# Encoder layer on one core: a reordered front, two decay buffers, raw router transposes, and the rows of an expert laid over all partitions

## The reference

```python
# x: (1, 512, 1024) for each sequence, mem: (1, 256, 1024)
P = rms_norm(x, norm_mix) @ w_in          # z, xbc, dt, q, k, v, pool columns
x = x + concat(ssd_heads, neighbourhood_attention, pool) @ w_out
x = x + memory_cross_attention(rms_norm(x, norm_xa), rms_norm(mem, norm_mem))
x = x + hier_moe(rms_norm(x, norm_ffn))
```

## Time and profile before

| what | value |
|---|---|
| median of 3 runs | 1175.89 us (1174.95 to 1176.49) |
| the profiled execution | 1172.96 us |
| its span in the trace | 1170.9 us |
| mean granted TensorE clock | 0.938 |
| busy PE, PEld | 1016.6, 810.3 us |
| busy DVE, ACT, POOL | 784.6, 466.5, 294.0 us |
| chain that ended last, by engine | PE 42%, DVE 13%, DMA 12%, issue 9%, ACT 6% |
| DMA | 197.40 MB, mean 169 GB/s |

### The profile page before, as it was taken

One profiled execution on the slowest core, in us unless ns is written; L12 is line 12 of the kernel. 1 busy time (PEld: TensorE's weight loads), 2 busy tenths in 40 slices (PEclk: granted clock), 3 DMA queues, 4 the chain that ended last, 5 costly groups with the idle time before them and its releaser, 6 DMA issues.

```text
span 1170.9 us, 13975 instructions
## 1 busy us (share of the span) xinstructions
PE 1016.6 (87%) x5029; PEld 810.3 (69%) x5029; DVE 784.6 (67%) x1251; ACT 466.5 (40%) x849; POOL 294.0 (25%) x346
## 2 busy tenths in 40 slices
PE   5798898998898999999979999756999998889982
PEld 4576676867677778788867888655777766666661
DVE  4436776777677677873455676457988787877771
ACT  4123343323235423421233343234666565564640
POOL 2223214321341222200110111004355233232212
PEclk9898999897898989899989999867999999999997
DMA  6132223121131523315120112735999989999952
GB/s 228 46 108 63 81 90 120 46 81 55 47 103 65 174 82 127 108 63 198 43 72 18 55 55 104 310 136 196 351 368 371 372 349 372 344 357 343 350 209 85
DMA packets 63397, 197.40 MB, mean 169 GB/s; under 512 B 16417, under 2 KB 22977, under 8 KB 50913
## 3 DMA queue, kind: packets, MB, share of 16 engines
q1 hardware_dynamic: 43344, 152.73, 35.9%
q0 software_dynamic: 18688, 39.52, 9.5%
q10 hardware_dynamic: 1296, 4.26, 0.9%
HBM read 190.16 MB, written 37.75 MB: 195 GB/s over the span
## 4 chain that ended last, share of the span: by engine, by line
PE 42%; DVE 13%; DMA 12%; issue 9%; ACT 6%; POOL 3%; ACTq 0%; POOLq 0%; DVEq 0%
DMA edr<-w_e_down 11%; PE bank L946 7%; PE bank L947 7%; PE bank L948 7%; PE gu_ps L946 3%; PE gu_ps L948 3%; PE gu_ps L947 3%; PE y_ps L1327 2%; PE bank L1131 2%; DVE egl L1728 2%; PE bank L1013 2%; PE xg_ps L1292 1%; ACT dec L1573 1%; ACT prob L1591 1%; PE bank L1263 1%
## 5 line engine op out<-in xcount | busy, mean ns | idle before, releaser
L946 PE MATMUL bank<-Wh,hTh 128*128 128x512 f32 x384 | 159.2, 415 | 7.9 <-issue 6.7
L947 PE MATMUL bank<-Wl,hTh 128*128 128x512 f32 x384 | 154.2, 401 | 0.0
L948 PE MATMUL bank<-Wh,hTl 128*128 128x512 f32 x384 | 153.9, 401 | 0.0
L1728 DVE TENSOR_TENSOR egl<-egr,ghi 128x2048 fp32r<-128x2048 f32 x64 | 143.9, 2288 | 14.7 <-ACT ghi L1397 14.7
L1397 ACT ACTIVATE ghi<-egr 128x2048 fp32r<-128x2048 f32 x64 | 119.6, 1931 | 0.0
L946 PE MATMUL gu_ps<-ghi,xgH 128*128 128x512 f32 x256 | 104.3, 408 | 1.4 <-DVE xgL L2093 1.4
L948 PE MATMUL gu_ps<-ghi,xgL 128*128 128x512 f32 x256 | 101.2, 395 | 0.0
L947 PE MATMUL gu_ps<-egl,xgH 128*128 128x512 f32 x256 | 100.9, 394 | 0.0
L946 PEld LDWEIGHTS bank<-Wh,hTh 128*128 128x128 f32 x384 | 75.5, 197 | 24.4 <-issue 7.4
L948 PEld LDWEIGHTS bank<-Wh,hTl 128*128 128x128 f32 x384 | 74.9, 195 | 16.6
L947 PEld LDWEIGHTS bank<-Wl,hTh 128*128 128x128 f32 x384 | 75.1, 196 | 15.6 <-issue 0.5
(11 more groups left out here) (325 smaller groups left out, 2243.3 us busy)
## 6 DMA issues: line engine op xcount, KB each, us to landing
egr<-w_e_gate SPq DMA_DIRECT2D x32, 1024.0 KB, 20.7
egr<-w_e_up SPq DMA_DIRECT2D x32, 1024.0 KB, 23.7
edr<-w_e_down SPq DMA_DIRECT2D x32, 1024.0 KB, 24.3
raw<-w_in SPq DMA_DIRECT2D x50, 256.0 KB, 3.1
xn<-w_in SPq DMA_DIRECT2D x22, 256.0 KB, 3.0
x_sb<-x_prompt SPq DMA_DIRECT2D x8, 512.0 KB, 6.1
partial_rows<-x_sb ACTq DMA_DIRECT2D x8, 512.0 KB, 2.6
ffn_rows<-xn_ffn POOLq DMA_DIRECT2D x8, 512.0 KB, 2.9
```

Of the source, the lines that this page charges most:

```text
L946: pe.matmul(dst, ah, bh, start=first, stop=False)
L947: pe.matmul(dst, ah, bl, start=False, stop=False)
L948: return pe.matmul(dst, al, bh, start=False, stop=last)
L1728: tt(egl[n % 4][:, a, :, :], egr[n % 4][:, a, :, :], ghi[n % 2][:, a, :, :].bitcast(F32), ALU.subtract)\
```

## The change

In words: (1) At the start the gain is loaded behind the first weight, hT 1 stands before norm 3 and hT 3 within the first head step; TensorE's wait for the constants moves to dtp 0. (2) Of a convolution ScalarE does the first product (from the bank, semaphore `conv_in`), and the tanh with the last product becomes a step `act` behind the next convolution; the steps around them are put in another order, and dt is split in two. (3) `dec` gets a second buffer where the attention's probabilities lie, with two new waits for that place; sdec is two chunks ahead; xdt and the normalisation (`yn`) are steps of their own; gating stands before the state's update. (4) The gain for xa shares the semaphore of mem. (5) The router's transposes read `x_sb` before normalisation; `router_w` is multiplied once by the gain, the logits by `rs`; the end of the loop is in another order, and VectorE copies the last half of `hf`. (6) The one-hot rows compare with `iota_s`, by which rank r goes to partition 8 (r mod 16) + r div 16.

```diff
-                   ("norm", "mix", 2), ("w", U_QK, 2), ("norm", "mix", 3), ("w", U_QK, 3)]
-            tl += [("hT", "mix", i) for i in range(1, TPS)]
+                   ("norm", "mix", 2), ("w", U_QK, 2), ("hT", "mix", 1), ("norm", "mix", 3), ("w", U_QK, 3),
+                   ("hT", "mix", 2)]
...
+            heads[0].insert(1, ("hT", "mix", 3))
...
-        mixed([[u[0]], [conv[4], na1[0]], [conv[5], conv_t[4]] + (ssd_groups(s - 1)[-1] if s else []),
-               [na2[0], u_t[0], u[1], nav[0]]], quarters(u0 + U_XS))
-        mixed([[na1[1], conv[0]], [conv[1], conv_t[0], na2[1]]], quarters(u0 + U_Z))
-        tl += [u_t[1], ("dtv", s), norm[0], conv[2], nav[1], conv_t[1], na1[2], norm[1], conv[3], conv_t[2]]
-        mixed([[z[0], h_t[0], na2[2]], [z[1], h_t[1], norm[2], nav[2], na1[3]],
-               [z[2], h_t[2], ("dt", s), conv_t[3], norm[3], na2[3]], [z[3], ("sback", s, 3), nav[3], h_t[3]]],
+        act = [("act", s, m) for m in range(6)]
+        mixed([[u[0], na1[0]], [conv[4]], [act[4], conv[5], conv_t[4]] + (ssd_groups(s - 1)[-1] if s else []),
+               [act[5], na2[0], u_t[0], u[1], nav[0]]], quarters(u0 + U_XS))
+        mixed([[na1[1], conv[0]], [act[0], conv[1], conv_t[0], na2[1]]], quarters(u0 + U_Z))
+        tl += [act[1], norm[0], conv[2], conv_t[1], nav[1], act[2], na1[2], norm[1], conv[3], conv_t[2], u_t[1], ("dtv", s)]
+        mixed([[z[0], act[3], h_t[0], na2[2], ("dtw", s)], [z[1], h_t[1], norm[2], nav[2], na1[3], ("dt", s)],
+               [z[2], conv_t[3], h_t[2], norm[3], na2[3]], [z[3], ("sback", s, 3), nav[3], ("sback", s, 2), h_t[3]]],
...
+        else:
+            tl += [("hT", "ffn", i - 1), ("xsn", i + 1)] + ranked[:1] + [("norm", "ffn", i - 1), ("xo", i), ("router", i - 1)]
+            tl += ranked[1:]
+    i = NT - 1
+    tl += [("xs2", i), ("hT", "ffn", i - 1), ("xav", i), ("topk", i - 2), ("norm", "ffn", i - 1), ("router", i - 1),
+           ("rank", i - 2), ("slots", i - 2), ("pre", 0), ("topk", i - 1), ("xo", i), ("rank", i - 1), ("hT", "ffn", i),
+           ("slots", i - 1), ("norm", "ffn", i), ("router", i), ("pre", 1), ("topk", i), ("rank", i), ("slots", i)]
...
-    back = [[("sback", s, 1), dec[0]]]
-    return back + [[y[0]], [dec[1], out[0]], [y[1]], [dec[2], out[1]], [y[2]], [dec[3], out[2]], [y[3]], [out[3]]]
+    groups = [[("sback", s, 1), dec[0], x[0]], [dec[1]]]
+    for c in range(TPS):
+        groups.append([y[c]] + x[c + 1:c + 2])
+        groups.append([yn[c]] + dec[c + 2:c + 3] + [out[c]])
...
+        decays = [dec, nc.alloc_sbuf_tensor_at("dec1", [P, 2, SSD_H, P], F32, offset=at["prob"])]
...
-                if step == ("norm", "mix", 0):
+                if step == ("w", U_QK, 0):
                     sp.dma_start(gain[:, :], row(dram["norm_mix"], D)).then_inc(gain_ld["mix"], 16)
...
-                if kind == "init":
+                if step == ("dtp", 0):
                     pe.wait_ge(const_ld, 16 * N_CONST)
...
+                    if st == "ffn":
+                        pe.wait_ge(x2, 2 * i + 2)
+                    src = x_sb[:, i, :] if st == "ffn" else normed(st, i)
...
+                    act.activation(cacc[:, k % 2, :], pb(step)[:, :], ACT.Identity, scale=cwh[:, m, 1:2],
+                                   bias=cbh[:, m:m + 1]).then_inc(conv_in, 1)
...
+                        if step[1] == 0:
+                            wait_full(act, ("sy", SEQS - 1, TPS - 1), 0)
...
+                    if step == ("norm", "ffn", 0):
+                        tt(router_w[:, :, :], router_w[:, :, :], per_head(g_ffn, NL), ALU.mult).then_inc(router_g, 1)
...
-                    link(ts(acc, b[:, :], cwh[:, m, 1:2], cbh[:, m:m + 1], ALU.mult, ALU.add))
+                    dve.wait_ge(conv_in, k + 1)
...
+                    if c == 1:
+                        wait_full(dve, ("nav", s, 3))
...
+                    if s and m == 0:
+                        wait_full(dve, ("sy", s - 1, TPS - 1), 0)
...
-                    tt(logits[:, i, :], pb(step)[:, 0:NL], router_b[:, :], ALU.add).then_inc(is_free(step), 1)
+                    stt(logits[:, i, :], pb(step)[:, 0:NL], rs[:, k:k + 1], router_b[:, :], ALU.mult, ALU.add)\
...
-                        ins = ts(oneh_p[:, c * NT + i, :], iota_p[:, :], rk[:, c, i:i + 1], None, ALU.is_equal)
+                        ins = ts(oneh_p[:, c * NT + i, :], iota_s[:, :], rk[:, c, i:i + 1], None, ALU.is_equal)
...
+                        pool.iota(iota_s[:, :].rearrange("p (a b) -> p a b", a=16), [[1, 16], [16, 8]], base=0,
+                                  channel_multiplier=0, allow_small_or_imprecise_dtypes=True).then_inc(r_pool, 1)
...
-                elif kind == "hT" and step[1] == "ffn":
-                    i = step[2]
+                elif kind == "router":
+                    i = step[1]
                     pool.wait_ge(xn_done, 1 + nth("norm", "ffn", i))
                     pool.dma_start(hn_dram[i * P:(i + 1) * P, :], xn_ffn[:, :]).then_inc(hn_st, 16)
```

More of the change, by code:

```diff
@@ L56 @@
 N_INIT = 8
-N_RPOOL = 5
+N_RPOOL = 6
 ROUND = 2.0 ** 23
@@ L166, in ssd_groups @@
 def ssd_groups(s):
-    dec, y, out = ([(kind, s, c) for c in range(TPS)] for kind in ("sdec", "sy", "sout"))
-    back = [[("sback", s, 1), dec[0]]]
-    return back + [[y[0]], [dec[1], out[0]], [y[1]], [dec[2], out[1]], [y[2]], [dec[3], out[2]], [y[3]], [out[3]]]
+    dec, x, y, yn, out = ([(kind, s, c) for c in range(TPS)] for kind in ("sdec", "xdt", "sy", "yn", "sout"))
+    groups = [[("sback", s, 1), dec[0], x[0]], [dec[1]]]
+    for c in range(TPS):
+        groups.append([y[c]] + x[c + 1:c + 2])
+        groups.append([yn[c]] + dec[c + 2:c + 3] + [out[c]])
+    return groups
 def bank_uses(step):
@@ L630, in encoder_layer @@
         init_a = sem("init_a")
-        gain_ld = {st: sem(f"gain_ld_{st}") for st in ("mix", "mem", "xa", "ffn")}
+        gain_ld = {st: sem(f"gain_ld_{st}") for st in ("mix", "mem", "ffn")}
         conv_sum = sem("conv_sum")
+        conv_in = sem("conv_in")
         conv_th = sem("conv_th")
@@ L1130, in _ @@
                         for dr in range(2):
-                            last = pe.matmul(b[:, hc], dec[:, dr, h, :], xdt[:, dr, hc], start=dr == 0, stop=dr == 1)
+                            last = pe.matmul(b[:, hc], decays[c % 2][:, dr, h, :], xdt[:, dr, hc], start=dr == 0, stop=dr == 1)
                     last.then_inc(is_full(step, 0), 1)
@@ L1445, in _ @@
                         dst = normed(st, i)
-                        if before_it:
+                        if st == "xa" and before_it:
                             wait_full(act, before_it[-1], 1)
-                        else:
+                        elif not (st == "ffn" and i):
                             wait_raw_used(act, plan.last_in[2 if st == "xa" else 3])
@@ L1463, in _ @@
                     i = step[2]
-                    for half in range(2):
+                    for half in range(1 if i == NT - 1 else 2):
                         wait_full(act, step, half)
@@ L1822, in _ @@
                     ins.then_inc(conv_sum, 1)
+                elif kind == "act":
+                    m, k = step[2], nth("conv", *step[1:])
                     dve.wait_ge(conv_th, k + 1)
@@ L1889, in _ @@
                         link(tt(y1[:, :], y1[:, :], y2[:, :], ALU.add))
+                        wait_full(dve, step, 0)
+                        tt(y1[:, :], y1[:, :], pb(step, 0)[:, :], ALU.add).then_inc(is_free(step, 0), 1)
+                        wait_released(dve, step, 0)
+                        dve.wait_ge(z_ld, 16 * (k + 1))
+                        tt(y1[:, :], y1[:, :], zg[:, :], ALU.mult).then_inc(y_done, 1)
                     j = 3 if kind == "sy" else 0
@@ L1908, in _ @@
                         wait_released(dve, step, j)
[L1909 to L1919 removed]
+                elif kind == "yn":
+                    dve.wait_ge(yrs_done, nth(*step) + 1)
+                    for g in range(SSD_G):
+                        r = slice(256 * g, 256 * g + 256)
+                        ins = ts(y2[:, r], y1[:, r], yrs[:, g:g + 1], None, ALU.mult)
+                    ins.then_inc(yn_done, 1)
                 elif kind == "sdec":
@@ L2299, in _ @@
                         wait_mixed(pool)
-                    pool.dma_start(GAIN[step[1]][:, :], bass.AP(dram[name].tensor, 0, [[0, P], [1, D]])).then_inc(gain_ld[step[1]], 16)
+                    pool.dma_start(GAIN[step[1]][:, :], bass.AP(dram[name].tensor, 0, [[0, P], [1, D]])).then_inc(gain_ld["ffn" if step[1] == "ffn" else "mem"], 16)
                     if step[1] == "ffn":
@@ L2358, in _ @@
                     ins.then_inc(u_win, 1)
+                    pool.wait_ge(u_win, 1 + nth(*step))
                 elif kind == "uT":
```

94 lines of the change are left out of this document (46 added, 48 removed).

## The result

The changed kernel takes 1140.41 us (median of four runs, 1137.49 to 1148.31) against 1176.19 (four runs, 1174.95 to 1177.24): a ratio of 0.9709 with a 95% interval of 0.9666 to 0.9752, faster by 35.8 us. The forecast was 1108 with a range of 1082 to 1136: right sign, half the size, outside the range.

What follows compares the result with a forecast made beforehand. It took TensorE to bound the kernel, busy 1016.6 of 1170.9 us, with its waits and lowered clock to gain. 7.5 + 22 + 16 + 4 + 12 + 6 = 67.5 off 1172.96, plus 2.93 to the median, gave 1108 us; range 1082 to 1136.

Steps and rivals of the forecast that it cites:

- Start, 7.5: Kernel start: TensorE's initial wait of 6.66 us and 2 of clock saved, less about 1 waiting for hT 3: 7.5 us.
- The 0 for the gain's DMA: Start: loading the gain one weight later costs 0, plus or minus 1, as the first transposes wait anyway.
- Convolution and attention, 22: Convolutions and neighbourhood attention, twice: lighter VectorE work and an earlier first softmax save 22 us, between bounds 10 and 37.
- What is late next is VectorE: Convolutions and attention: VectorE's softmaxes share its queue, and ScalarE's new first product stands before exponentials that others wait for.
- VectorE's 18 us of relief: Convolutions: VectorE loses 9.7 + 8.4 = 18 us, from products moved to ScalarE and tanh waits filled with other work.
- Chunks, 16: SSD chunks, twice: decay two chunks ahead removes L1131's 12.9 us wait; half of the upper bound 32 counted, 16 us.
- The 2 us of clock: TensorE: each wait of over 2 us costs 2 us more, since work behind it runs at a lower clock.
- Rival B: Before the experts VectorE becomes the bound; convolutions give 10, chunks 6: 1130 us. Chance 0.21.
- Loop and tail, 16: Router: transposes no longer wait for normalisation; 4 us in the loop and 12 in the tail.
- Experts, 6: Experts: the new row places fill the engines used evenly, 0.3 us x 19 = 6 us; half of the places stay empty.
- The 108%: Experts: load if all rows sat on eight engines, 67.2 + 40.4; taken to say nearly all rows do.
- The upper bound of 27: Experts: rows perfectly spread over the engines save 1.4 us for each of 19 experts, 27 us.

Runs made afterwards that it cites:

- the groups were undone: Changed kernel with nine chunk groups in the old arrangement (y and its normalisation in one group), second decay buffer kept: 1123.22 us, ratio 0.9581.
- the old places: Changed kernel with an expert's rank r on partition r again: 1144.97 us, ratio 0.9755.
- a true spread: Changed kernel with the iota placing rank r on DMA engine r mod 16, so 64 rows are four on each of 16 engines: 1106.24 us, ratio 0.9438.

## Why the prediction was wrong, point by point

- **Start, 7.5.** Right in kind; measured 10.2 and 11.0. No wait is left at the first q/k projections, and in the first 60 us the clock is 1.00 instead of 0.94. The 0 for the gain's DMA did not hold: the first normalisation waits for the gain until 8.98 us, where it began at 6.67, and the first transposes come 2.3 us later. The first projection still starts 2.4 us earlier (18.88 for 21.25), since three transpose steps stand in front of it and not four.
- **Convolution and attention, 22.** The term that was mis-sized. Leads of 8.5 and 5.2 us (9.5 and 5.4 in the second profile) make 14 to 15, of which 2.9 and 4.8 go at the backward states (2.8 and 4.3), together with the first chunk's work: about 7 net. "What is late next is VectorE" was right, but I credited VectorE's 18 us of relief as TensorE's time. The waits of L1063 stayed at 9.4 of 10.6, and the split bought nothing: at the longest VectorE made two weights' rests (L1764, from 104.92 to 107.93) in front of act's last product. What paid was L1172's wait, 9.5 to 1.2, by the place of the first softmax (7.6 us in time, counted with nearly half of 9.5). The move of backward state 2 I had not costed at all; its xw now stood right behind POOL's gate store.
- **Chunks, 16.** The step that failed: "so L1131's 12.9 goes" with the normaliser's wait "usable, by the step of its own". The first happened; the second was the loss. The normalisation got a step of its own one group later, behind the heads' work and the weights' rests on VectorE and directly in front of its reader. In the profile the chunks gave back 5.0 and 4.9 us (5.1 and 1.8 in the second) instead of giving 16: 23 to 26 us of error here, and 17.6 of it came back when the groups were undone. Even then the chunks won only 3.5 and 5.4 us, so 16 was too much for any of the orders tried. The 2 us of clock taken for each wait over 2 us were too few for the longest: behind the 8.11 us wait some 7 us went (an estimate, half of the 13.85 us at the lower clock). Rival B's addition had a moved wait, but in front of L1131; it went behind it.
- **The reason of rival B** did not hold. VectorE is busy 48.2 and 49.9 of 60 us, but the same load in another order is 17.6 us faster. Its time, 1130, was the nearest of the cases to 1140, by luck and not by its cause.
- **Loop and tail, 16.** Right by the profiles: 18.0 and 18.1. L1013's 14.5 us in the router are down to 2.1.
- **Experts, 6.** Right in kind. The places changed and half of the engines still carry nearly all rows; measured 0 to 2 between the profiles before and after, 4.1 between the medians with old and new places in the new front (there 373.6 against 369.0 and 367.1 us of experts). The 108% that I took as a proof was a hint: with the old places the same sum is 70.8 + 2 x 21.1 = 113% from 900 to 1050 us, so the shares are not exact enough for "just above 100". The two distances that I read were a little high: the last of the eight matmuls is 0.8 us behind the first, so 9.72 and 11.31, not 9.8 and 11.36. The upper bound of 27 was too low: a true spread gives 34.6. In the profiles it is 369.0 - 333.5 = 35.5; 19 experts at 11.31 - 9.72 are 30 of it, and the rest lies at the end, where I had counted nothing: from the last expert's first transpose to the end of the span it is 39.0 us instead of 43.9.
- **The tests named.** Held: L946, L1131, w_e_down over 80 us (101.6), L1013 nearly (2.1). Failed: L1055 and L1172 under 6 (10.6), the clock at 0.95 (0.89 and 0.82), experts 11.0 to 11.1 us apart (11.21, by a little), and the first gate matmul, under 30 us earlier, which I had named as being wrong altogether.
- **The range.** It ended at 1136 because no case had a part that loses more than its own term. B took the chunks from 16 to 6; a reordering can go below zero, and its lower end should have been a loss of the size of the waits that it creates.

## What to carry to other kernels

A late step is not free because its engine has room: ask what stands ahead of it in its queue and how much work its reader has in front of it. Here one such move cost 17 us, and only without it could be seen that a decay made two chunks ahead gained nothing. Where one indirect DMA moves fewer rows than it has partitions, choose the partitions by the engine that serves them; a single iota gave 34.6 and 34.9 us in two different kernels. The fastest version found has the change's start, softmax place and router, the old chunk groups, backward state 2 behind the transposes and the even spread: 1087.59 us, 0.9267 (0.9251 to 0.9282) of the kernel before and 53 us under the changed one.

## What the runs showed of the hardware

- The first 64 rows of an indirect DMA on eight engines or on sixteen, by the rule above: 352 or 412 GB/s from 900 to 950, and the first case's mean DMA share of 0.93 alone looks like a bound that is nearly reached. What gave it away was the sum of the two queues' shares at the experts' pace, and what settled it was the run with the spread.
- A long wait of TensorE costs beyond its length: behind one of 8.11 us the granted clock was 0.50 for the next 14 us of work, in which the 32 matmuls of a chunk took 7.09 us instead of 3.68.
- The kernel before stays within 0.5% (1171.3 to 1177.1 in seven runs), the changed one within 1.3% (1133.9 to 1148.3 in eight), and the version with backward state 2 moved within 0.2% (1086.5 to 1088.8 in four). Where that comes from stays open; it was not tried.
